# A decoder layer on one core: second buffers in the scan, other first loads, another last pass, denser decode grains

## The chip, the core and the metric

The kernel runs on one core of a Trainium2 chip. The metric is the device time of one execution in microseconds (us); three runs of the kernel before give a median and a range.

## What is computed

One step of a hybrid decoder layer, for a prompt of 512 tokens and for 8 sequences of 8 new tokens (64 sample tokens), 576 tokens in all, model width 2048, everything in 32-bit floats:

```python
mod = silu(c) @ w_ada + b_ada;  shift, scale, gate = split(mod, 3)
h = rmsnorm(x, g_pre) * (1 + scale) + shift
q, k, v, z_a, z_b, xbc, dt_raw, r_a, r_b = split(h @ w_in)
# A: three groups of dilated window attention, 8 heads of 128, (window, step) =
#    (128, 1), (512, 4), (2048, 16); the samples attend to cached keys and values too
o_a = sum_g softmax_g(lse_g) * attention_g(q, k, v);  p_a = (o_a * silu(z_a)) @ w_o_a
# B: convolution of width 4 on xbc, then a chunked state-space scan: 8 groups of 4 heads
y, new_states = ssd(xs * dt, dt * a, b, c, old_states)      # plus D skip, silu(z_b), norm
p_b = yn @ w_o_b
out = (sigmoid(r_a) * p_a + sigmoid(r_b) * p_b) @ w_o
y_out = x + gate * rmsnorm(out, g_post)
```

The outputs are y for prompt and samples, the key/value windows shifted by the new rows (some 170 MB copied), and the new convolution and scan states.

## The kernel before, in words

All large products go through 209 **units** (UNITS): a unit is one slab of 128 output columns for all 576 tokens. Units 0 to 110 are q, k, v, the gates z and r, and dt; 111 to 160 (from BLOCK0 = 111) are the slabs x and s of the scan's groups and two r; 161 to 176 (A0) multiply by w_o_a and have half the depth; then come 16 units B (w_o_b) and 16 units O (w_o). In a unit the weights are split in two parts: ACT copies the slab `raw` to `wh` (`high(u)`, line 821), POOL subtracts (`wl = raw - wh`, line 779, the tile w_lo), and PE does 3 matmuls of 288 columns for each of 16 depth steps and each of two token halves (`multiply`, lines 1156 to 1158). wh and wl have two buffers each. `raw` has three slots of 1 MB; SP loads unit u's weights (`weights`, line 432) when the low part of the unit three places before has been made (`slot_free`).

Everything else is laid over the units by **half units**: each engine's program walks `half` = 0 to 417, and what is due at a half unit stands in its queue behind that half's part of the unit. All queues run in order. SP is some halves behind its own weights (`seen`).

- **Modulation.** 32 slabs of w_ada go first, through the three slots of `raw` (`modulation`, line 1089); the small vectors v_in are waited for by PE ahead of them (line 1077). Columns of x are normalised and split (`normed`, `low`, and ACT's loop at 811 to 813), and PE starts unit 0 after all 16 (`pe.wait_ge(a_lo, KT)`).
- **Decode grains.** The samples' attention to cached keys and values is on DVE: 96 key grains and 96 value grains (`key_grain`, `value_grain`), each a product (line 1488 or 1517) and a sum (1491 or 1520) over 2048 columns. Their chunks of 1 MB come in two buffers `kd`, loaded one half ahead. `grain_half(n) = n * 16 // 17` puts 17 grains on 16 halves, the keys from half 22, the values from half 117. Then the new rows follow from half 208 (NEWS0): scores, a merge of maxima, and at half 217 (NEWV0) `value_news`, eight products (line 1534) and sums (line 1538) in one go. PE's `fold_halves` (line 1218) follows after unit 111.
- **Prompt attention** runs from half 61 to half 225 in 32 steps (head and residue class) of five halves each, with scores on PE (line 1194), a mask and a maximum on DVE (1613 to 1618), the exponential on ACT (906), transposes (1201) and the value product (1211) on PE, and 1625 and 1631 on DVE.
- **The scan.** Group g has steps o = 0 to 21, one per half from BASE[g] on, 12 halves (6 units) apart; from o = 8 on the last group goes at half that pace. PE's `outputs(g, i)` (o = 7, 9, ... 15) multiplies old states `h0T` (512 columns, line 1282), which SP loads at o = 4, 8, 10 and 12 into one buffer. For the new states POOL scales `h0` (1 MB of old states to SBUF; line 767) at o = 6 and 12, DVE adds (line 1761), and SP stores it (line 611), waits for the store, and loads the next half into the same buffer (line 606). POOL does its scan steps of a unit before the next unit's w_lo:

```python
for u in range(NU):
    pool.wait_ge(hi, u + 1)
    ...
    nc.gpsimd.tensor_tensor(wl[:, u % 2, ...], raw[...], wh[...], ALU.subtract).then_inc(lo, 1)
    ...
    for half in (2 * u, 2 * u + 1):
        for g, o in ssm_steps(half):
            ssm(g, o)
```

- **The last pass.** Units O are transposed back on PE (`back`), copied to `outs` by DVE (`copy_out`, 1854), and squared on ACT four units at a time (`squares`). After the last one DVE does `outs * rstd * gg` (line 1919) and `+ x` (line 1925) for each of five token tiles, and SP stores each.

## Time and profile before

| what | us |
|---|---|
| runs (three): median, range | 3415.59, 3413.01 to 3420.86 |
| the profiled execution: its time, its span | 3431.45, 3429.7 |
| busy PE, DVE, POOL, ACT | 3095.8, 1978.9, 1103.1, 867.8 |
| mean granted clock of TensorE | 0.944 of full speed |
| first matmul of unit 0; last matmul of unit 208 | 142.4; 3393.3 |

PE is busy for 90% of the span, DVE for 58%, POOL for 32%, ACT for 25%. Busy PE time is modelled from pipelined matmuls, and at half clock the same work shows as more busy time, so a stretch is read with its granted clock beside it. The profiled execution is 15.9 us above the median of the runs.

### The profile page before, as it was taken

Reading aid. Unit: us, or ns where it says so; the run is one execution under the profiler, and the core shown is the slowest. Engines: PE = TensorE matmul, PEld = TensorE weight load, DVE = VectorE, ACT = ScalarE, POOL = GpSimd, SP = SyncE. Lnnn points to the kernel's source line nnn. Section 1 sums busy time; section 2 is a strip of 40 time slices with the busy share of each in tenths; the row PEclk is TensorE's granted clock in tenths of the full one; section 3 lists DMA queues with packets and bytes.
Section 4 is the critical chain, followed back from the end, with each engine's and each line's share of the span. In section 5 each row is a group of like instructions: output and inputs, shape, how many; then the busy total and the mean of one; then the engine's idle time right before and its main releaser. Section 6 shows DMA issues by size and latency. Waiting matters only on the chain. (4 is left out here: it accounts for less than half of the span.)

```text
span 3429.7 us, 53566 instructions
## 1 busy us (share of the span) xinstructions
PE 3095.8 (90%) x23404; PEld 2985.7 (87%) x23404; DVE 1978.9 (58%) x1996; ACT 867.8 (25%) x1045; POOL 1103.1 (32%) x367
## 2 busy tenths in 40 slices
PE   5799999999999999989997988898887889999995
PEld 4698999899999999979996978887887878899995
DVE  3201799788857778777866466656646655211204
ACT  2111122232232222222231322322322232211221
POOL 0123333233323332233332333423324333333331
PEclk7799999999999999999998999999998989999998
DMA  8777777453537675555664455345445445766533
GB/s 304 258 260 262 304 277 254 162 198 119 172 129 256 233 266 193 194 229 207 250 230 168 176 192 176 134 175 210 155 161 203 170 148 179 266 248 243 212 137 111
DMA packets 222256, 704.94 MB, mean 206 GB/s; under 512 B 28659, under 2 KB 131819, under 8 KB 172459
## 3 DMA queue, kind: packets, MB, share of 16 engines
q1 hardware_dynamic: 159478, 471.33, 39.4%
q0 software_dynamic: 5248, 174.60, 12.6%
q10 hardware_dynamic: 57296, 55.59, 4.8%
q8 instruction: 185, 3.03, 0.4%
q14 instruction: 49, 0.40, 0.0%
HBM read 630.85 MB, written 245.17 MB: 255 GB/s over the span
## 5 line engine op out<-in xcount | busy, mean ns | idle before, releaser
L1156 PE MATMUL acc<-act,w_hi 128*128 128x288 f32 (+1 forms) x6432 | 1962.9, 305 | 141.8 <-POOL w_lo L779 134.0
L1157 PE MATMUL acc<-act,w_hi 128*128 128x288 f32 (+1 forms) x6432 | 1922.3, 299 | 0.0
L1158 PE MATMUL acc<-act,w_lo 128*128 128x288 f32 (+1 forms) x6432 | 1920.9, 299 | 0.0
L779 POOL TENSOR_TENSOR w_lo<-w_raw,w_hi 128x2048 fp32r<-128x2048 f32 (+1 forms) x209 | 968.8, 4636 | 1859.5 <-ACT w_hi L821 1844.1
L1156 PEld LDWEIGHTS acc<-act,w_hi 128*128 128x128 f32 (+1 forms) x6432 | 1233.2, 192 | 174.7 <-POOL w_lo L779 138.3
L1157 PEld LDWEIGHTS acc<-act,w_hi 128*128 128x128 f32 (+1 forms) x6432 | 1233.2, 192 | 2.8
L1158 PEld LDWEIGHTS acc<-act,w_lo 128*128 128x128 f32 (+1 forms) x6432 | 1230.4, 191 | 0.9
L821 ACT ACTIVATE w_hi<-w_raw 128x2048 fp32r<-128x2048 f32 (+1 forms) x209 | 384.1, 1838 | 407.6 <-PE acc L1158 235.4
L1517 DVE TENSOR_TENSOR side<-side 128x2048 f32<-128x2048 f32 x96 | 279.6, 2913 | 150.0 <-DMA side<-in_vals_t 142.1
L1488 DVE TENSOR_TENSOR side<-side 128x2048 f32<-128x2048 f32 x96 | 308.7, 3216 | 83.1 <-DMA side<-in_keys_t 79.0
L887 ACT ACTIVATE ev<-acc 128x576 f32<-128x576 f32 x160 | 103.7, 648 | 893.3 <-PE acc L1158 889.9
L1520 DVE TENSOR_REDUCE side<-side 128x32 f32<-128x2048 f32 x96 | 219.5, 2286 | 3.3
L1491 DVE TENSOR_REDUCE side<-side 128x16 f32<-128x2048 f32 x96 | 219.5, 2286 | 3.3
L767 POOL TENSOR_TENSOR side<-side 64x1024 f32<-64x1024 f32 x32 | 63.4, 1982 | 252.7 <-DMA side<-in_state_ssm 251.5
L1688 DVE SCALAR_TENSOR_TENSOR side<-ev,vec,side 128x511 f32<-128x511 f32 (+2 forms) x96 | 126.6, 1319 | 3.4
L1677 DVE COPY side<-side 128x24 f32<-128x24 f32 x32 | 38.9, 1214 | 151.6 <-ACT ev L887 83.6
L1826 DVE TENSOR_TENSOR ev<-acc,side 128x576 f32<-128x576 f32 x16 | 12.1, 758 | 174.7 <-PE acc L1158 174.7
L968 ACT ACTIVATE side<-side 128x512 f32<-128x512 f32 (+1 forms) x40 | 23.5, 588 | 346.0 <-DVE side L1698 346.0
L906 ACT ACTIVATE side<-side,small 128x768 f32<-128x768 f32 x32 | 30.0, 938 | 268.4 <-DVE small L1618 268.4
L1282 PEld LDWEIGHTS ps_s<-side 128*128 128x128 f32 x256 | 37.0, 222 | 61.6 <-DMA side<-in_state_t 59.5
L1282 PE MATMUL ps_s<-side 128*128 128x8 f32 x256 | 39.9, 283 | 55.9 <-DMA side<-in_state_t 55.9
L1086 PE MATMUL ps_s<-w_raw,side 128*32 128x128 f32 x1536 | 68.6, 335 | 20.1 <-DMA w_raw<-in_w_ada_t 20.1
(232 smaller groups left out, 2077.9 us busy)
## 6 DMA issues: line engine op xcount, KB each, us to landing
w_raw<-in_w_in_t SPq DMA_DIRECT2D x160, 1024.0 KB, 8.0
out_s_kv<-in_cache_a_w POOLq DMA_DIRECT2D x80, 1632.0 KB, 9.0
side<-in_keys_t SPq DMA_DIRECT2D x52, 1024.0 KB, 7.7
side<-in_vals_t SPq DMA_DIRECT2D x52, 1024.0 KB, 8.3
w_raw<-in_w_ada_t SPq DMA_DIRECT2D x48, 1024.0 KB, 7.7
out_s_kv<-in_cache_a_w POOLq DMA_DIRECT2D x24, 1344.0 KB, 8.3
w_raw<-in_w_o_b_t SPq DMA_DIRECT2D x16, 1024.0 KB, 7.6
w_raw<-in_w_o_t SPq DMA_DIRECT2D x16, 1024.0 KB, 8.7
```

The source lines that it names most:

```text
L779: nc.gpsimd.tensor_tensor(wl[:, u % 2, 0:kt, 0:cols], raw[:, s % 3, 0:kt, 0:cols], wh[:, u % 2, 0:kt, 0:cols].bitcast(F32), ALU.subtract). ...
L821: nc.scalar.activation(wh[:, u % 2, 0:kt, 0:cols], raw[:, s % 3, 0:kt, 0:cols], ACT.Copy).then_inc(hi, 1)
L887: nc.scalar.activation(ev[0:cols, c, :].rearrange("p (a n) -> p a n", a=2), banks, func).then_inc(evac, 1)
L1156: nc.tensor.matmul(out, wh[:, c, k, 0:cols], high, start=(k == 0), stop=False)
L1157: nc.tensor.matmul(out, wh[:, c, k, 0:cols], low, start=False, stop=False)
L1158: mm = nc.tensor.matmul(out, wl[:, c, k, 0:cols], high, start=False, stop=(k == kt - 1))
L1282: mm = nc.tensor.matmul(Y[:, 2 * P + j * SAMP + b * NT:2 * P + j * SAMP + (b + 1) * NT], h0T[:, b4 * P:(b4 + 1) * P], xa[:, 3, SEQ + b * N ...
L1488: TT(prod.rearrange("p (r e) -> p r e", e=E), kd[:, j % 2, :].rearrange("p (r e) -> p r e", e=E), qd[:, gi % 2, t, :].unsqueeze(1).broadca ...
L1491: TR(sc[:, t, gi, 16 * c:16 * c + 16], prod.rearrange("p (r e) -> p r e", e=E), AX, ALU.add).then_inc(d_sum, 1)
L1517: TT(prod.rearrange("p (e r) -> p e r", r=64), kd[:, j % 2, :].rearrange("p (e r) -> p e r", r=64), sc[:, t, gi, 0:64].unsqueeze(1).broadc ...
L1520: TR(og[:, 0 if gi == 2 else 1, t, 32 * c:32 * c + 32], prod.rearrange("p (e r) -> p e r", r=64), AX, ALU.add).then_inc(d_sum, 1)
L1688: STT(xp[:, lag:], ev[:, c, 0:SEQ - lag], w[3 - lag], xp[:, lag:], ALU.mult, ALU.add).then_inc(cv, 1)
```

## The change

**SP, POOL and PE in the scan.** POOL makes the low part of the *next* unit before the scan steps of this one (`weights_low`). From unit 111 to 166 weights use two slots of `raw` instead of three; the third holds a second `h0` (for the second half of a group's states) and two further `h0T` buffers (for the last group they lie in a part of `side`). `h0T` is loaded at o = 3, 5, 7 and 9, `h0` at o = 4 and 8, and no load waits for the store just issued. The decay rows (`log_decays`) move from o = 1, 3, 5, 7, 9 to 1, 3, 6, 8, 10.

**First loads.** The small vectors are loaded before the first slabs of w_ada and waited for behind the second; unit 0's weights are loaded before the last two slabs and made into wh before the last column is split; PE waits for each split column of unit 0 by itself.

**Decode grains.** Eight grains on seven halves, and the new rows' values one t at a half.

**Last pass.** The gate and norm weights are multiplied in `copy_out`; ACT squares every unit from PSUM; at the end one DVE operation a tile is left, and the samples' tile goes to ACT and POOL.

```diff
-SLOT_OF = {entry: NADA + i for i, entry in enumerate(STREAM)}
+ADA_SLOT = [n if n < NADA - 2 else n + 1 for n in range(NADA)]
+SLOT_OF = {entry: NADA + i if i else NADA - 2 for i, entry in enumerate(STREAM)}
...
+    _few = _kind == "u" and BLOCK0 <= _n < A0 + 4
+    if _few:
+        _slot = _next[1] % 2
...
+        _slot = _next[0] % 3
...
 def grain_half(n):
-    return n * 16 // 17
+    return n * 7 // 8
...
-NEWV0 = NEWS0 + 9
-FOLD0 = NEWV0 + 6
+NEWV0 = NEWS0 + 13
+FOLD0 = NEWV0 + 9
...
+        def h0(g, j):
+            buf = (xa_free if g == SG - 1 else spare)[:, 0:1024] if j else side[:, 6912:7936]
...
+        def hT_buf(g, k):
+            return k % 3 if g == SG - 1 else (4 * g + k) % 3
...
+            def slot_free(s):
+                kind, n = ENTRY[BEFORE[s]]
...
+                if kind == "u":
+                    sp.wait_ge(lo, n + 1)
+                    if KINDS[n] == "A":
+                        sp.wait_ge(ma_d, n - A0 + 1)
+                    if s == SLOT_THIRD:
+                        sp.wait_ge(yt, 5 * (SG - 1))
+                        sp.wait_ge(s_out, 32 * (SG - 1))
...
-            for n in range(3, NADA):
-                sp.wait_ge(ada_used, n - 2)
...
+            for n in range(NADA):
+                s = ADA_SLOT[n]
+                if n == NADA - 2:
+                    weights(0)
+                if s >= 3:
+                    slot_free(s)
...
+            def carried(g, k):
+                older = [(gg, kk) for gg in range(g + 1) for kk in range(4) if (gg, kk) < (g, k) and hT_buf(gg, kk) == hT_buf(g, k)]
+                if older:
+                    sp.wait_ge(yt, 5 * older[-1][0] + older[-1][1] + 1)
+                spare_free(g, hT_buf(g, k))
+                sp.dma_start(h0T(g, k), A["state_t"][g, k]).then_inc(hT_in[hT_buf(g, k)], 16)
...
             def old_states(g, j):
+                after(sp, s_out, 16 * (2 * g + j - 1))
+                spare_free(g, j)
...
-                if o in (1, 3, 5, 7, 9):
-                    log_decays(g, o // 2)
+                if o in (1, 3, 6, 8, 10):
+                    log_decays(g, (1, 3, 6, 8, 10).index(o))
...
-                if o in (4, 8, 10, 12):
-                    k = (4, 8, 10, 12).index(o)
-                    after(sp, yt, 5 * g + (k if k else -1))
-                    sp.dma_start(h0T, A["state_t"][g, k]).then_inc(hT_in, 16)
-                if o == 4 and g == 0:
+                if o in (3, 5, 7, 9):
+                    carried(g, o // 2 - 1)
+                if o == 4:
                     old_states(g, 0)
-                if o == 11:
+                if o == 8:
+                    old_states(g, 1)
+                if o == 12:
                     new_states(g, 0)
-                    sp.wait_ge(s_out, 16 * (2 * g + 1))
-                    old_states(g, 1)
-                if o == 17:
+                if o == 18:
                     new_states(g, 1)
-                    if g + 1 < SG:
-                        sp.wait_ge(s_out, 16 * (2 * g + 2))
-                        old_states(g + 1, 0)
...
-                return max(0, 2 * min(u, NGATE + 2) - 4, 2 * u - (8 if u < A0 + 3 else 4))
+                lag = 8 if u < BLOCK0 else 6 if u < A0 + 2 else 2 if u < A0 + 4 else 4
+                return max(0, 2 * min(u, NGATE + 2) - 4, 2 * u - lag)
...
             sent = 0
+            weights_low(0)
             for u in range(NU):
+                if u + 1 < NU:
+                    weights_low(u + 1)
...
+            pool.wait_ge(f_s, 1)
+            pool.wait_ge(c_in, 80)
+            nc.gpsimd.tensor_tensor(outs[4][0:SAMP, :], outs[4][0:SAMP, :], xT[4][0:SAMP, :], ALU.add).then_inc(f_p, 1)
...
+            for k in range(KT - 1):
+                split_h(k)
             high(0)
+            split_h(KT - 1)
...
-                v = u - O0
-                if v >= 5 and v % 4 == 1:
-                    squares(v // 4 - 1)
-            squares(3)
+                if u >= O0 + 2:
+                    squares(u - O0 - 2)
...
+            nc.scalar.activation(outs[4][0:SAMP, :], outs[4][0:SAMP, :], ACT.Copy, scale=fstat[0:SAMP, 4, 2:3]).then_inc(f_s, 1)
...
-                if half == NEWV0:
-                    value_news()
+                if NEWV0 <= half <= NEWV0 + NT:
+                    value_news(half - NEWV0)
...
-                TC(outP[:, :, cols], src.rearrange("p (t c) -> p t c", t=4)).then_inc(o_c, 1)
+                TT(outP[:, :, cols], src.rearrange("p (t c) -> p t c", t=4), gateP[:, cols].unsqueeze(1).broadcast_to((P, 4, P)),
+                   ALU.mult).then_inc(o_c, 1)
...
-            for t in range(5):
...
-                STT(outs[t][0:n, :], outs[t][0:n, :], fstat[0:n, t, 2:3], gg[0:n, :], ALU.mult, ALU.mult).then_inc(f_s, 1)
...
-                TT(outs[t][0:n, :], outs[t][0:n, :], xT[t][0:n, :], ALU.add).then_inc(f_d, 1)
+                STT(outs[t], outs[t], fstat[:, t, 2:3], xT[t], ALU.mult, ALU.add).then_inc(f_d, 1)
```

With this the values begin at half 111, the new rows at half 196, their values at half 209, and PE folds after unit 109.

SP's queue over one group of the scan, about the loads of group 1 (`in_state_t` is h0T, `in_state_ssm` and `out_s_ssm` are h0, `w_in_t` a unit's weights, `csT` the decay rows). Before:

```order
L455 DMA w_raw<-in_w_in_t 128x2048
L630 DMA side<-in_state_t 128x512
L648 DMA ynT<-side 128x2x576
L602 DMA side<-csT 128x4x128
L455 DMA w_raw<-in_w_in_t 128x2048
L630 DMA side<-in_state_t 128x512
L611 DMA out_s_ssm<-side 128x8x128
L606 DMA side<-in_state_ssm 128x8x128
L455 DMA w_raw<-in_w_in_t 128x2048
L630 DMA side<-in_state_t 128x512
L602 DMA side<-csT 128x4x64
```

Now:

```order
L668 DMA side<-in_state_t 128x512
L487 DMA w_raw<-in_w_in_t 128x2048
L653 DMA side<-csT 128x4x128
L674 DMA w_raw<-in_state_ssm 128x8x128
L711 DMA ynT<-side 128x2x576
L668 DMA w_raw<-in_state_t 128x512
L487 DMA w_raw<-in_w_in_t 128x2048
L653 DMA side<-csT 128x4x128
L487 DMA w_raw<-in_w_in_t 128x2048
L679 DMA out_s_ssm<-side 128x8x128
L653 DMA side<-csT 128x4x64
```

Before, each load of h0 stands right behind the store of h0 (and waits for its landing); now it stands a unit or more ahead of the store, and h0T goes out ahead of a unit's weights, not after them.

DVE's queue at the new rows' values (L1534 and L1538 before, L1620 and L1624 now, are product and sum of one t; L1613 to L1631 before are prompt attention). Before:

```order
L1534 TENSOR_TENSOR side<-side 128x1536
L1538 TENSOR_REDUCE side<-side 128x128
L1534 TENSOR_TENSOR side<-side 128x1536
L1538 TENSOR_REDUCE side<-side 128x128
L1534 TENSOR_TENSOR side<-side 128x1536
L1538 TENSOR_REDUCE side<-side 128x128
L1534 TENSOR_TENSOR side<-side 128x1536
L1538 TENSOR_REDUCE side<-side 128x128
L1525 TENSOR_TENSOR side<-side 128x1024
L1621 RECIPROCAL small<-small 128x1
L1631 TENSOR_TENSOR side<-ps_w,side 128x128
L1625 TENSOR_SCALAR side<-ps_w,small 128x128
```

Now:

```order
L1687 TENSOR_TENSOR side<-side 128x1024
L1620 TENSOR_TENSOR side<-side 128x1536
L1624 TENSOR_REDUCE side<-side 128x128
L1620 TENSOR_TENSOR side<-side 128x1536
L1624 TENSOR_REDUCE side<-side 128x128
L1712 TENSOR_SCALAR side<-ps_w,small 128x128
L1620 TENSOR_TENSOR side<-side 128x1536
L1624 TENSOR_REDUCE side<-side 128x128
L1700 TENSOR_TENSOR side<-ps_s,side 128x512
L1701 TENSOR_TENSOR side<-ps_s,side 128x256
L1703 TENSOR_REDUCE small<-side 128x1
L1705 TENSOR_SCALAR small<-small 128x1
```

Before, the eight t stand in a row and the attention's L1621 and L1631, for which PE waits, behind them; now attention's work stands between them.

## Rows read from the trace of the kernel before

**Rows 1.** Waits, whole span: who waited for whom, us, times, longest.

```profile
PE acc L1156 <- POOL w_lo L779: 134.0, 27, 9.5
...
PE ps_s L1282 <- DMA side<-in_state_t: 55.9, 15, 9.6
...
PE ps_w L1211 <- DVE side L1631: 24.1, 1, 24.1
```

**Rows 2.** Stretches: us; PE, PEld, DVE, ACT, POOL; PEclk, DMA, GB/s.

```profile
2183.50:2302.70 119.20, 104.93 (x731) 98.34 (x728) 75.46 (x128) 32.46 (x44) 41.74 (x17) 0.91 0.50 175
...
2668.20:2683.40 15.20, 15.20 (x111) 14.08 (x109) 9.18 (x17) 4.90 (x9) 6.98 (x3) 1.00 0.00 1
...
2683.40:2708.80 25.40, 16.54 (x124) 15.81 (x122) 16.96 (x25) 11.96 (x16) 9.33 (x4) 0.90 0.53 172
...
2464.20:2482.70 18.50, 18.13 (x119) 16.82 (x119) 13.30 (x29) 3.64 (x5) 5.58 (x3) 0.89 0.89 323
...
2728.60:2745.60 17.00, 16.88 (x129) 15.56 (x127) 11.65 (x24) 3.69 (x5) 4.59 (x2) 1.00 0.56 201
...
2264.40:2283.70 19.30, 15.57 (x125) 15.16 (x124) 13.85 (x20) 5.38 (x8) 8.47 (x4) 1.00 0.43 162
...
2283.70:2302.70 19.00, 18.92 (x132) 17.29 (x130) 9.93 (x16) 2.86 (x4) 5.49 (x2) 0.91 0.42 161
...
1937.00:2828.30 891.30, 766.88 (x5412) 719.76 (x5410) 530.62 (x915) 249.94 (x332) 308.82 (x128) 0.91 0.49 174
```

**Rows 3.** Timeline of POOL, 2191 to 2245 us: start, us, work, [idle before].

```profile
2214.05 3.89 POOL L767 TENSOR_TENSOR side<-side 64x1024 f32<-64x1024 f32 x2 [15.70 <-DMA side<-in_state_ssm]
...
2218.02 5.50 POOL L779 TENSOR_TENSOR w_lo<-w_raw,w_hi 128x2048 fp32r<-128x2048 f32 x1
```

**Rows 4.** Timeline of the SP queue, 2197 to 2232 us.

```profile
2199.55 1.22 SPq L611 DMA_DIRECT2D out_s_ssm<-side  x1
...
2209.64 0.38 SPq L606 DMA_DIRECT2D side<-in_state_ssm  x1
```

**Rows 5.** DVE L1688 in 1937-2828.3 us as a group; one of it.

```profile
L1688 DVE SCALAR_TENSOR_TENSOR side<-ev,vec,side 128x511 f32<-128x511 f32 (+2 forms) x84 | 113.4, 1350 | 3.0
...
2267.98 5.10 DVE L1688 SCALAR_TENSOR_TENSOR side<-ev,vec,side 128x510 f32<-128x510 f32 x1
```

**Rows 6.** Busy time at the fold (columns as in 2); DVE groups there.

```profile
1818.70:1859.10 40.40, 16.31 (x110) 13.47 (x109) 30.19 (x16) 2.57 (x2) 7.64 (x2) 0.70 0.24 88
...
L1534 DVE TENSOR_TENSOR side<-side 128x1536 f32<-128x1536 f32 x8 | 25.6, 3204 | 0.2
```

**Rows 7.** Busy time, key and value stretches (columns as in 2).

```profile
432.00:597.00 165.00, 165.00 (x1245) 164.53 (x1245) 161.29 (x54) 40.18 (x45) 57.55 (x12) 1.00 0.76 268
...
700.00:1000.00 300.00, 299.79 (x2237) 297.23 (x2236) 240.63 (x141) 87.09 (x105) 101.19 (x21) 1.00 0.44 148
...
589.00:630.00 41.00, 33.57 (x237) 32.90 (x237) 29.01 (x18) 9.73 (x12) 9.04 (x2) 0.88 0.48 177
```

**Rows 8.** DVE groups: keys 432-597 us, values 1000-1400 us.

```profile
L1488 DVE TENSOR_TENSOR side<-side 128x2048 f32<-128x2048 f32 x27 | 99.7, 3694 | 2.9 <-DVE side L1491 0.5
...
L1517 DVE TENSOR_TENSOR side<-side 128x2048 f32<-128x2048 f32 x52 | 143.6, 2762 | 94.0 <-DMA side<-in_vals_t 86.8 <-ACT side L925 6.2
```

**Rows 9.** Timelines of ACT and POOL, 125 to 147 us.

```profile
132.40 0.68 ACT L813 ACTIVATE act<-ev 128x576 fp32r<-128x576 f32 x1 [6.56 <-DVE ev L1438]
...
135.80 3.69 ACT L821 ACTIVATE w_hi<-w_raw 128x2048 fp32r<-128x2048 f32 x2
...
137.77 9.02 POOL L779 TENSOR_TENSOR w_lo<-w_raw,w_hi 128x2048 fp32r<-128x2048 f32 x2 [136.79 <-ACT w_hi L821]
```

**Rows 10.** Last pass: DVE timeline from 3399.5 us; DMA issues from 3400 us.

```profile
3400.59 2.35 DVE L1919 SCALAR_TENSOR_TENSOR side<-side,small 128x2048 f32<-128x2048 f32 x1
...
3402.97 2.29 DVE side L1925
...
out_y_prompt<-side SPq DMA_DIRECT2D x4, 1024.0 KB, 3.9
```

More of the change, by code:

```diff
@@ L306, in phase_all @@
         csr2 = side[:, 5888:6912].rearrange("p (a h n) -> p a h n", a=2, h=4)
-        h0 = side[:, 6912:7936].rearrange("p (b n) -> p b n", b=NB)
-        h0T = side[:, 7936:8448]
+        spare = raw[:, 2, :, :].rearrange("p k n -> p (k n)")
         St = side[:, 8448:8704]
@@ L332, in phase_all, with hT_loads, h0T @@
         xds = side[0:SAMP, 18168:18424].rearrange("p (h q) -> p h q", h=4)
+        xa_free = side[:, 11232:13536]
+        def h0(g, j):
+            buf = (xa_free if g == SG - 1 else spare)[:, 0:1024] if j else side[:, 6912:7936]
+            return buf.rearrange("p (b n) -> p b n", b=NB)
+        def hT_buf(g, k):
+            return k % 3 if g == SG - 1 else (4 * g + k) % 3
+        def hT_loads(g, k):
+            return sum(1 for gg in range(g + 1) for kk in range(4) if (gg, kk) <= (g, k) and hT_buf(gg, kk) == hT_buf(g, k))
+        def h0T(g, k):
+            i = hT_buf(g, k)
+            return (xa_free if g == SG - 1 else spare)[:, 512 + 512 * i:1024 + 512 * i] if i else side[:, 7936:8448]
         X, Y, Z = (ps_t, ps_w), ps_s[:, 0:512], ps_s[:, 512:1024]
@@ L412, in _ @@
             sp.dma_start(ident[:, :], A["ident"]).then_inc(c_in, 16)
-            for n in range(3):
-                sp.dma_start(raw[:, n, :, :].rearrange("p k n -> p (k n)"), A["w_ada_t"][(n % 2) * KT + n // 2]).then_inc(w_in[n], 16)
             r = 0
@@ L535, in decode_loads @@
                     new_rows(2, 0, n_in)
[L536 removed]
+                if half == NEWS0 + 10:
                     sp.wait_ge(sm_e, 1 + 2 * NT)
@@ L770, in ssm, with weights_low @@
                     pool.wait_ge(sn_m, 4 * g + 2 * j + 2)
-            sent = 0
-            for u in range(NU):
+            def weights_low(u):
                 cols = unit_cols(u)[1]
@@ L810, in _, with split_h @@
             nc.scalar.activation(root[0:SAMP, 4:5], ssq[0:SAMP, 4:5], ACT.Sqrt, bias=eps[0:SAMP, :], scale=1.0 / D).then_inc(root_done, 1)
-            for k in range(KT):
+            def split_h(k):
                 act_e.wait_ge(h_f, k + 1)
@@ L1117, in _ @@
                     modulation(n)
+                    if n == 1:
+                        vectors()
                     if n:
@@ L1150, in multiply @@
                 sl = slice(half * HALF, (half + 1) * HALF)
-                first = {A0: SPLIT_OA, B0: SPLIT_Y, O0: SPLIT_M}.get(u) if half == 0 else None
+                first = {0: 0, A0: SPLIT_OA, B0: SPLIT_Y, O0: SPLIT_M}.get(u) if half == 0 else None
                 for k in range(kt):
-                    if first:
+                    if first is not None:
                         pe.wait_ge(a_lo, first + k + 1)
@@ L1526, in merge, with value_news @@
                 dve.wait_ge(o_add, n)
-            def value_news():
-                dve.wait_ge(n_in, 64)
-                dve.wait_ge(o_add, 3)
-                for t in range(NT):
+            def value_news(t):
+                if t == 0:
+                    dve.wait_ge(n_in, 64)
+                    dve.wait_ge(o_add, 3)
+                if t < NT:
                     dve.wait_ge(n_sum, 6 + t)
@@ L1586, in softmax @@
                     dve.sem_inc(sm_x, 1)
-                if half == NEWS0 + 8:
+                if half == NEWS0 + 12:
                     dve.wait_ge(sm_w, 96)
@@ L1807, in gate_a @@
                 s, c = SLOT_OF["u", u], u % 2
-                ra = raw[:, s % 3, :, :].rearrange("p k n -> p (k n)")[:, KA * P:KA * P + TOK]
+                ra = raw[:, SLOT[s], :, :].rearrange("p k n -> p (k n)")[:, KA * P:KA * P + TOK]
                 dve.wait_ge(used, u + 1)
-                dve.wait_ge(ra_in[s % 3], 16 * sum(1 for v in range(A0, u + 1) if SLOT_OF["u", v] % 3 == s % 3))
+                dve.wait_ge(ra_in[SLOT[s]], 16 * sum(1 for v in range(A0, u + 1) if SLOT[SLOT_OF["u", v]] == SLOT[s]))
                 if n >= 2:
@@ L1903, in _ @@
                     copy_out(u - 2 - O0)
-                if half == 2 * NU - 8:
+                if half == 2 * O0 + 3:
                     dve.wait_ge(fin_in, 16 * (2 + NB))
```

194 lines of the change are left out of this document (110 added, 84 removed).

## The prediction, made before the changed kernel was run

> **What bounds the kernel now.** I read the table of waits first, then busy time cut by the unit, then timelines of the queues in the worst stretch, and last the two ends. Over the span PE waits 134.0 us for POOL's w_lo (27 times, at most 9.5), 55.9 us for the scan's old states in_state_t (15 times), and once 24.1 us for DVE's L1631 [rows 1]. So PE is the bound, and what can be won is where it waits for a part or a load. Most of that lies in one regular pattern. From 1937 to 2828.3 us PE is busy for 766.9 of 891.3 us, at a granted clock of 0.91 [rows 2].
>
> One group of the scan (six units) runs from 2183.5 to 2302.7 us: 119.2 us [rows 2]. To see what it would take unhindered I take each kind of unit where its part is busy almost all the time: x,0 15.2 us; x,1 16.5 (the busy part of a unit that took 25.4, so 8.9 us of it were idle); x,2 18.13 less the 11% of 18.5 us that its clock of 0.89 cost, 16.1; x,3 16.9; s,0 15.6; s,1 18.9 less 9% of 19.0, 17.2 [rows 2]. Together 97.5 us. The stretch holds 5412 matmuls and the group 731, so 7.4 groups [rows 2]; 7.4 x 97.5 = 722, and 169 us are lost, 23 a group.
>
> The chain behind it shows in two queues. SP issues the store of h0 (L611) at 2199.55 and, after waiting for its landing, the load of the next h0 (L606) at 2209.64 [rows 4]: ten microseconds in which the one buffer is a store's source. POOL stands idle for 15.70 us for that load, scales from 2214.05 in two pieces of 3.89 us in all, and only then makes the next unit's w_lo, from 2218.02 on, in 5.50 us [rows 3]. PE waits for that w_lo. The loads of h0T come late in the same way, since they stand behind SP's wait. After a gap PE also runs slower for a while: its granted clock is 1.00 in the undisturbed x,0 unit and 0.90 in the x,1 unit with its 8.9 idle us [rows 2], so a gap costs more than its length.
>
> **The scan, part by part.** The change takes the store's landing out of SP's way (a second h0 in the third weight slot, loads at o = 4 and 8, stores at 12 and 18), and puts w_lo of the next unit ahead of POOL's scan steps. Both have to hold, and I think that both do: a load has four halves, some 30 us, where now it has the time between a store's landing and o = 12. h0T goes out at o = 3 to 9 into three buffers, ahead of need by about two halves (16 us), where a state load of twice that size takes 4.4 us from its issue at 2209.64 to POOL's start at 2214.05 [rows 3, 4]. What is left at risk is the weights: between units 111 and 166 they have two slots, so a unit's weights are loaded after the w_lo of the unit two places before. w_lo takes 4.5 to 5.5 us, a 1 MB transfer 3.9, w_hi 1.85, the next w_lo 4.5 again [rows 3, 9, 10]: 15 to 16 us, against units of 15.2 to 17.2. POOL works a unit ahead, so this chain turns on POOL's own round and not on PE's, but there is no slack to speak of in an x,0 unit. I keep 3 us lost a group for it (bounds: 0, and 8.9 as at the x,1 unit now), and 7 us once where A begins and the lag of SP's side jobs changes. Kept: 7.4 x 3 + 7 = 29. **Scan: 169 - 29 = -140 us** (ends -169 and -100).
>
> **Fold.** value_news puts eight products of 3.2 us and their sums in one go on DVE; L1631 stands behind them, and the window from 1818.7 to 1859.1 is one unit that took 40.4 us with PE busy 16.3 at a clock of 0.70 [rows 1, 6]. At full clock those 16.3 us would be about 14 (estimate, between 16.3 x 0.70 = 11.4 and 16.3). One t a half leaves attention's work between them. **Fold: -26 us.** Nine halves instead of one carry about 5 us more of DVE work each; DVE is busy 30.2 of those 40.4 us now, so the same work, spread over nine halves of 7 to 8 us, is cover that suffices unless attention's steps fill them (then a few gaps of 2 to 3 us; end -15).
>
> **Denser grains.** This is the term that goes against the change. In the key stretch before attention, DVE is busy 161.3 of 165 us while PE is never idle, and 27 grains start in it [rows 7, 8]: 6.0 us a grain, nearly full. Eight on seven halves instead of seventeen on sixteen is 7.6% more, 29.0 grains in the same 165 us, or 173 us of work. Over the 39 halves from 22 to 61 it adds three grains, so 18 us of lag, when the first attention step comes; already now PE is idle 7.4 of the 41 us there, at a clock of 0.88 [rows 7]. Behind that, halves are longer: from 700 to 1000 us DVE is busy 240.6 of 300 with 40 grains [rows 7], and 3 more at 5 to 6 us make 256, so that the lag is worked off. I take 12 us more gap once, plus 3 for the clock after it. In the value stretch DVE waits 86.8 us for chunks while it makes 52 grains [rows 8]; there the rate is set by loads and DVE has time. **Grains: +15 us** (ends -10, if the chunk waits that reach PE become fewer, and +45, if three steps stall in place of one).
>
> **The first loads.** Now the last column is split at 132.40 in 0.68 us, w_hi of units 0 and 1 follow at 135.80 (3.69 for two), w_lo of unit 0 is done 4.5 us after 137.77, and PE starts at 142.4 [rows 9]. With w_hi of unit 0 ahead of the last split it can start at 133.1, w_lo ends at 133.1 + 1.85 + 4.5 = 139.5: 2.8 us. The vectors no longer stand before PE's first sum; another 1.2 us from the stream of w_ada (ends 5, and -3 since unit 0's megabyte, 3.9 us [rows 10], now goes ahead of the last two slabs). **Head: -4 us.**
>
> **The last pass.** Five tiles of 2.35 + 2.29 us [rows 10] are 23.2 us; four of 2.35 are 9.4: 13.8 less. The samples' tile costs 1.9 us on ACT (as a w_hi) and at most 4.5 on POOL (as a w_lo) beside them [rows 9]. But the four stores of 1 MB take 3.9 us each [rows 10]; one after another they are 15.6 us, and then only 9 us are saved. **Tail: -10 us** (ends -13.8 and -9). The Trainium skill, "SBUF — State Buffer", section "Who interferes with whom", says that a DVE instruction with two SBUF inputs contends with a GpSimd instruction that reads SBUF, and that the loser waits for the whole instruction; by it POOL's addition of 4.5 us would stand in DVE's way and the saving would be 9.3. That the gate's multiplication moves into the copies from PSUM, and the squares to one unit at a time, I cost at nothing: beside them ACT has little but one w_hi of 1.85 us a unit [rows 9] and DVE no grains or scan any more; without that cover `back`, which now waits for the squares of two units before, would hold PE for a microsecond or so in each of 16 units, 16 us.
>
> **Sum.** -140 - 26 + 15 - 4 - 10 = -165 on the profiled execution's 3431.45, so 3266.5. That execution is 15.9 us above the median 3415.59; the forecast for the median is **3250 us**.
>
> **Rivals.** *The prefetch does not come early* (the change does not do what it says): SP's queue runs in order, each h0T now waits for an earlier `yt`, and two weight slots leave SP waiting for POOL; a late weight load then holds back every state load. For it: the 15 to 16 us round above. Against: w_lo is now made ahead of the scan's steps. If half of the 169 us stays, 85 instead of 29, the time is 3306. *DVE becomes the bound of the scan.* It is busy 75.5 of the 119.2 us of a group [rows 2], which would be 75.5 of 97.5. One L1688 took 5.10 us where the mean of 84 is 1.35 [rows 5], at a time when POOL was busy 8.47 us in one unit with its scaling and w_lo [rows 2]; such a block on DVE did not stop PE then, since PE was late itself. With the slack gone, two blocks of 8.5 us a group and 3 us of clock would, 20 us x 7.4 = 148, less the 22 already kept: 3376. The rule of the Trainium skill named above, in "SBUF — State Buffer", "Who interferes with whom", is this mechanism; the 5.10 us agrees with it, but is one instruction. *The denser grains never let DVE catch up* (the other side): prompt attention has 32 steps, and if DVE's lag stays above the two halves or so that a step can bear, each step stalls PE as the first one does now, 7.4 us and 2 of clock [rows 7]. It decides once DVE's work in the attention stretch passes its time, which needs 60 us more in 300 where I count 16. With 27 of the 32 steps stalled, 3250 - 15 + 27 x 9 = 3478, slower by 1.8%.
>
> **How the numbers follow.** Forecast 0.81, prefetch late 0.08, DVE the bound 0.05, grains' stall 0.03, others 0.03 (a new wait in the A units, most likely, 20 to 60 us above the forecast). The forecast's own range is 3205 to 3290: all of the scan's 29 us and a gain from the grains at one end, the scan at -100 at the other. With the first rival's 3306 it is 3200 to 3306. A measurement of this kernel tells about 0.2% (7 us) from no change; faster by more than that has all but the third rival, 0.96, the same 0.01, slower 0.03.
>
> **What would show it.** In the changed profile: POOL's wait for in_state_ssm and PE's for in_state_t gone or under 10 us together; a group of the scan at 98 to 103 us with a clock near 1.00; no wait of 24 us for the attention's product after unit 109; a first attention step with some 12 us more idle time than now; the first matmul near 138 us; 25 to 27 us from the last matmul to the end. The forecast is wrong if the scan's groups stay above 110 us, if PE waits for DVE at more than three attention steps, or if w_lo stays the largest releaser of PE with tens of waits.

## The result, and the profile after

The changed kernel takes 3334.84 us (median of four runs, 3333.79 to 3336.43) against 3418.23 for the kernel before in the same comparison (3413.01 to 3427.05): a ratio of 0.9754, interval 0.9732 to 0.9776. It is faster by 83 us; the forecast said 165, and the time lies above its range, which ended at 3306. The profiled executions, 3336.43 and 3431.45 us, differ by 95.0; of those 13 stem from the one before lying above its own median. The forecast's 165 was for this pair, so it missed by 70 us: 52 at the grains, 11 in the scan, 8 in the A units, and the rest smaller and partly against each other.

The table splits the two profiled executions at the first matmul of a unit. "Gap" is time in which PE did nothing.

| stretch | before | after | change | forecast |
|---|---|---|---|---|
| start to unit 0 | 142.4 | 130.0 | -12.4 | -4 |
| units 0 to 29 | 432.0 | 435.3 | +3.3 | 0 |
| units 30 to 60 | 477.0 (gap 13.1) | 509.2 (gap 36.1) | +32.2 | +15 |
| units 61 to 109 | 767.3 (gap 41.1) | 802.4 (gap 62.7) | +35.1 | (in the +15) |
| unit 110, the fold | 40.4 | 13.9 | -26.5 | -26 |
| units 111 to 160, the scan | 969.2 | 840.1 | -129.1 | -140 |
| units 161 to 176 (A) | 134.9 | 143.2 | +8.3 | 0 |
| units 177 to 208 | 430.4 | 430.3 | 0 | 0 |
| after the last matmul | 36.1 | 30.2 | -5.9 | -10 |

Busy time by stretch in the changed kernel (columns as in [rows 2]): units 30 to 60, 61 to 109, the fold's unit, units 116 to 160, and one group of the scan, the one after that of [rows 2]:

```profile
565.30:1074.50 509.20, 473.11 (x3415) 465.53 (x3412) 400.42 (x225) 137.49 (x177) 151.73 (x31) 0.96 0.49 172
1074.50:1876.90 802.40, 739.73 (x5289) 728.23 (x5289) 578.43 (x356) 215.04 (x241) 252.11 (x74) 0.96 0.57 206
1876.90:1890.80 13.90, 13.90 (x110) 11.76 (x110) 0.95 (x2) 1.54 (x1) 5.08 (x2) 1.00 0.54 199
1967.80:2730.90 763.10, 739.08 (x5419) 692.59 (x5418) 493.64 (x915) 245.47 (x326) 302.56 (x128) 0.98 0.59 202
2154.90:2256.70 101.80, 99.21 (x730) 92.90 (x730) 69.37 (x128) 32.57 (x44) 40.30 (x17) 0.98 0.57 197
```

The group that answers to 119.2 us at a clock of 0.91 now takes 101.8 at 0.98, and the fold's 24.1 us wait is gone [rows 2, 6]. But units 30 to 109, with their matmuls unchanged, are 67 us longer. PE's waits over the whole span of the changed kernel:

```profile
PE acc L1245 <- POOL w_lo L845: 79.0, 24, 10.6
...
PE ps_s L1290 <- ACT side L982: 22.4, 4, 13.9
PE ps_s L1393 <- DVE side L1834: 19.5, 7, 3.3
```

There is no wait for in_state_t any more and the 134.0 us for w_lo are 79.0 [rows 1], but these stand elsewhere: none in the scan's groups, most of it between units 30 and 114. L982 is the exponential of a prompt attention step. One of the forecast's signs of being wrong is there: w_lo is still PE's largest releaser, with 24 waits.

How w_lo, which is POOL's, comes late in an attention step can be followed at unit 51. DVE, then ACT, POOL and PE, each in its own timeline of the changed kernel (start, us, work, idle before and what ended it):

```profile
898.94 6.38 DVE L1573 TENSOR_TENSOR side<-side 128x2048 f32<-128x2048 f32 x1 [9.64 <-DMA side<-in_keys_t]
...
912.32 2.29 DVE L1573 TENSOR_TENSOR side<-side 128x2048 f32<-128x2048 f32 x1
914.65 2.29 DVE L1576 TENSOR_REDUCE side<-side 128x16 f32<-128x2048 f32 x1
916.85 0.35 DVE L1712 TENSOR_SCALAR side<-ps_w,small 128x128 f32<-128x128 f32 x1
917.11 2.29 DVE L1573 TENSOR_TENSOR side<-side 128x2048 f32<-128x2048 f32 x1
919.43 2.29 DVE L1576 TENSOR_REDUCE side<-side 128x16 f32<-128x2048 f32 x1
...
923.67 0.15 DVE L1705 TENSOR_SCALAR small<-small 128x1 f32<-128x1 f32 x1
```

```profile
923.86 0.94 ACT L982 ACTIVATE side<-side,small 128x768 f32<-128x768 f32 x1 [14.04 <-DVE small L1705]
...
924.79 1.89 ACT L897 ACTIVATE w_hi<-w_raw 128x2048 fp32r<-128x2048 f32 x1
```

```profile
926.76 4.51 POOL L845 TENSOR_TENSOR w_lo<-w_raw,w_hi 128x2048 fp32r<-128x2048 f32 x1 [23.59 <-ACT w_hi L897]
```

```profile
931.33 0.61 PE L1245 MATMUL acc<-act,w_hi 128*128 128x288 f32 x1 [3.09 <-POOL w_lo L845]
```

DVE, held by a chunk's load until 898.94, works off grains one behind the other and comes to the mask and maximum (the last is L1705) at 923.67. The first product took 6.38 us and not 2.29; POOL's w_lo, from 898.60 on for 4.58 us, ran beside it. ACT has stood for 14 us at the exponential, and w_hi of the next unit stands behind it in ACT's queue; POOL's w_lo waits for that, and PE for w_lo. The wait is charged to POOL, and the work behind it is the grains ahead in DVE's queue, together with the late chunk and the slow product; e4 below moves the grains and nothing else.

### The profile page after: what moved, and what is told of

It is laid out like the page before. It is cut to its first block, busy times and chain, and to the rows that moved or that the text cites. A ratio compares the mean times of both kernels' runs of the same rounds, so it can differ in the third digit from the quotient of the medians.

```text
span 3334.7 us, 53699 instructions
## 1 busy us (share of the span) xinstructions
PE 3082.8 (92%) x23404; PEld 2970.4 (89%) x23404; DVE 1931.1 (58%) x1990; ACT 883.3 (26%) x1166; POOL 1093.6 (33%) x368
## 4 chain that ended last, share of the span: by engine, by line
PE 59%; DVE 13%; DMA 10%; issue 9%; POOL 5%; ACT 2%; SPq 1%; ACTq 0%; DVEq 0%; POOLq 0%
PE acc L1245 18%; PE acc L1246 17%; PE acc L1247 17%; POOL w_lo L845 5%; DVE side L1602 3%; DVE side L1775 2%; DMA side<-in_vals_t 2%; DMA side<-in_state_conv_t 2%; DMA w_raw<-in_w_ada_t 2%; ACT w_hi L897 1%; PE ps_s L1172 1%; DMA side<-in_keys_t 1%; DVE side L1776 1%; DVE side L1605 1%; DVE side L1573 1%
## 5 line engine op out<-in xcount | busy, mean ns | idle before, releaser
L845 POOL TENSOR_TENSOR w_lo<-w_raw,w_hi 128x2048 fp32r<-128x2048 f32 (+1 forms) x209 | 955.2, 4571 | 2195.7 <-ACT w_hi L897 2195.5
L1602 DVE TENSOR_TENSOR side<-side 128x2048 f32<-128x2048 f32 x96 | 282.3, 2941 | 134.7 <-DMA side<-in_vals_t 132.7
L1573 DVE TENSOR_TENSOR side<-side 128x2048 f32<-128x2048 f32 x96 | 315.4, 3285 | 74.8 <-DMA side<-in_keys_t 70.6
L1775 DVE SCALAR_TENSOR_TENSOR side<-ev,vec,side 128x511 f32<-128x511 f32 (+2 forms) x96 | 171.2, 1783 | 3.4
L982 ACT ACTIVATE side<-side,small 128x768 f32<-128x768 f32 x32 | 30.0, 938 | 328.1 <-DVE small L1705 328.1
L1172 PE MATMUL ps_s<-w_raw,side 128*32 128x128 f32 x1536 | 66.2, 326 | 27.5 <-DMA w_raw<-in_w_ada_t 27.2
L1172 PEld LDWEIGHTS ps_s<-w_raw,side 128*32 128x32 f32 x1536 | 49.0, 130 | 35.8 <-DMA w_raw<-in_w_ada_t 22.0
L1764 DVE COPY side<-side 128x24 f32<-128x24 f32 x32 | 16.4, 514 | 108.8 <-ACT ev L963 62.9
L906 ACT ACTIVATE side<-ps_t 128x512 f32<-128x512 f32 x48 | 28.5, 594 | 145.5 <-PE ps_t L1257 145.5
L1776 DVE SCALAR_TENSOR_TENSOR side<-side,vec 128x64 f32<-128x64 f32 x96 | 60.8, 633 | 0.0
```

What stands on the lines that cost most here:

```text
L845: nc.gpsimd.tensor_tensor(wl[:, u % 2, 0:kt, 0:cols], raw[:, SLOT[s], 0:kt, 0:cols], wh[:, u % 2, 0:kt, 0:cols].bitcast(F32), ALU.subtract ...
L1172: mm = nc.tensor.matmul(ps_s[q:q + 32, (n % 2) * 512:(n % 2) * 512 + P], c32[:, k, :], raw[:, SLOT[src], k, :], start=(k < 4), stop=(k >= ...
L1573: TT(prod.rearrange("p (r e) -> p r e", e=E), kd[:, j % 2, :].rearrange("p (r e) -> p r e", e=E), qd[:, gi % 2, t, :].unsqueeze(1).broadca ...
L1602: TT(prod.rearrange("p (e r) -> p e r", r=64), kd[:, j % 2, :].rearrange("p (e r) -> p e r", r=64), sc[:, t, gi, 0:64].unsqueeze(1).broadc ...
L1775: STT(xp[:, lag:], ev[:, c, 0:SEQ - lag], w[3 - lag], xp[:, lag:], ALU.mult, ALU.add).then_inc(cv, 1)
```

## The experiments

All were timed in three rounds beside the kernel before (medians 3417.4, 3418.2, 3419.2 and 3413.8 us in the four comparisons). "Attention" is units 30 to 60 and 61 to 109, "fold" units 110 to 113, "scan" units 116 to 160, all from one profiled execution.

| kernel | median | ratio of medians (95% interval) | attention | fold | scan |
|---|---|---|---|---|---|
| before | | | 477.0 + 767.3 | 80.5 | 892.3 |
| after | 3334.8 | 0.9754 (0.9732-0.9776) | 509.2 + 802.4 | 52.2 | 763.1 |
| e1 before, dense grains | 3497.5 | 1.0234 (1.0213-1.0255) | 510.6 + 824.8 | 52.2 | 898.7 |
| e2 after, sparse grains | 3268.8 | 0.9563 (0.9544-0.9581) | 474.3 + 758.5 | 70.2 | 761.2 |
| e3 after, new rows later | 3312.3 | 0.9689 (0.9667-0.9712) | 509.9 + 777.0 | 53.9 | 759.7 |
| e4 after, attention first | 3232.7 | 0.9462 (0.9438-0.9485) | 477.2 + 728.8 | 52.2 | 760.8 |
| e5 after, POOL's old order | 3410.0 | 0.9971 (0.9957-0.9985) | 509.6 + 802.2 | 52.2 | 837.5 |
| e6 before, attention first | 3349.1 | 0.9795 (0.9775-0.9816) | 464.0 + 719.2 | 67.1 | 892.7 |
| e7 = e4, sparse | 3198.7 | 0.9356 (0.9336-0.9375) | 464.0 + 710.3 | 66.4 | 759.3 |
| e8 = e4, D weights, tail | 3219.7 | 0.9421 (0.9399-0.9442) | 475.7 + 734.4 | 52.2 | 761.4 |
| e9 before, POOL's new order | 3291.7 | 0.9627 (0.9608-0.9645) | 474.4 + 755.8 | 79.2 | 779.4 |
| e10 = e8, 12 grains on 11 | 3211.8 | 0.9397 (0.9381-0.9413) | 469.1 + 731.5 | 54.0 | 761.9 |
| e11 after, loose halves | 3302.8 | 0.9662 (0.9644-0.9680) | 495.0 + 779.2 | 52.2 | 764.0 |
| e12 = e7, tail | 3191.4 | 0.9342 (0.9309-0.9375) | 458.5 + 710.2 | 66.6 | 758.8 |

**e1, e2: what density costs.** One line in either kernel:

```diff
-    return n * 16 // 17
+    return n * 7 // 8
```

e1, on record before it ran: 

> The kernel before with eight grains on seven halves and nothing else changed (new rows, their values and the fold follow 12 halves earlier). Theory D (density is what the forecast mis-sized): units 30 to 109 get about 50 to 65 us longer, and the total is about 50 us above that of the kernel before, some 3465 us. Rival P (the forecast's +15 was right for the grains alone, and the added gaps of the changed kernel come from its new queue orders): about +15 us, 3430. Either way the scan's groups stay at 119 to 123 us.

e2 is the other way round (new rows' offsets as before, their values two a half): 

> The changed kernel with 17 grains on 16 halves; the new rows' values come two t at a half over four halves. Theory D: units 30 to 109 fall by 50 to 65 us, the total by about 55 us to 3280, with up to 10 us of gap back at the fold. Rival P: 3320, since most of the added gaps stay.

Both speak for density, and it cost more than I expected: +80 us on the kernel before, -66 without it in the changed one. The attention stretch is 91 us longer in e1 and 79 shorter in e2. The +15 of the forecast is too small by a factor of four to six (67, 79 or 91 us). In e1 the fold costs nothing, but the 27.6 us wait for L1625 stands at unit 103, which took 42.6 us:

```profile
1776.60:1819.20 42.60, 14.95 (x106) 14.47 (x105) 41.71 (x20) 3.21 (x2) 6.95 (x2) 0.71 0.36 139
```

DVE is busy for 41.71 of 42.60 us: the eight products and sums in one go hit whatever attention step follows. The changed kernel has nothing of the kind, so the spreading of the values, and not the earlier fold, took the 26 us away; in e2, with two t a half, 14.6 us of gap are back at unit 111.

**e4, e6: the place of attention in DVE's queue.** In e4 one call moves up, and nothing is added or left out; e6 does the same to the kernel before:

```diff
+                attention(half)
                 for n in grains.get(half - KEYS0, ()):
                     key_grain(n)
...
                     value_news(half - NEWV0)
-                attention(half)
```

> The changed kernel with attention's operations ahead of the grains of the same half on DVE. Theory B (gaps come from one or two grains, 5 to 14 us, in front of a step's operation): most gaps of units 30 to 109 go, 40 to 60 us less, some 3285. Rival: DVE then waits for PE's scores before it may start its grains, loses its lead, and the next half's operations are as late as before: 3325 to 3350.

> The kernel before with attention's operations ahead of the grains and of the new rows' values of the same half on DVE; nothing else. If the place of attention in DVE's queue is what makes the gaps of units 30 to 109 at the old density too, about 35 to 50 us less there (they have 53.7 us of gaps, some of which are waits for loads), 3370 to 3385 in total, the fold's gap and the scan as before. If those gaps come from a lag that attention's place does not change, within 10 us of 3417.

e4 is 102 us faster than the changed kernel (40 to 60 were expected), all of it in the attention stretch (-105.6), more than density had added. The rival, that DVE would lose its lead by waiting for PE, is out. e6 wins 69 us on the kernel before, at its old density, where 35 to 50 were expected. In the stretch of units 61 to 109, e6 reads:

```profile
1031.00:1750.20 719.20, 711.78 (x5273) 705.23 (x5273) 619.44 (x358) 214.69 (x239) 252.34 (x75) 1.00 0.67 244
```

DVE is busy for 86% of that stretch and PE loses 7 us; in the changed kernel DVE is busy for 72% and PE loses 63 (above). So DVE's mean load in the stretch does not tell how long PE waits. What counted was what stood ahead of attention's operations in its queue.

**e11: mean load or bursts.** As many grains on as many halves, but a half with two grains is moved by 0 to 4 halves to one in which attention has nothing for DVE:

```diff
+    double = {next(h for h in range(d, d + 5) if h < ATT0 or (h - ATT0) % 5 == 2) for d in range(base, base + 84, 7)}
```

> The changed kernel with as many grains on as many halves (96 on 84, twelve halves with two), but from half 61 on each half with two grains is moved on, by 0 to 4 halves, to one in which attention has no operation on DVE (the third of its five). Theory B (a half with two grains right in front of attention's operations makes the gaps, not the mean load): the gaps of units 61 to 109 fall from 62.7 us to 35 or less, with their clock 30 to 45 us less in all, 3290 to 3305. Rival M (the mean load of DVE): within 8 us of 3335.

The total came within the range of theory B, 32 us less, but not wholly in the way it says: the gaps of units 61 to 109 fall from 62.7 to 47.2 us, not to 35. So the doubled halves explain a part, about 37 of the 79 us between e2 and the changed kernel (14.2 in units 30 to 60, 23.2 in units 61 to 109). One long gap is left in e11, that of the next run.

**e3: one coincidence.** Two halves' shift of the new rows, their values and the fold:

```diff
-NEWS0 = VALS0 + grain_half(NGR) + 1
+NEWS0 = VALS0 + grain_half(NGR) + 3
```

> The changed kernel with the new rows two halves later (half 198 and not 196), so that the wait for their load does not stand ahead of the first operation of an attention step. Theory N (the longest added gap, 13.9 us at unit 99 and 5.5 behind it with their slow clock, is that wait's place): 15 to 23 us less, 3312 to 3320. Rival (DVE is late there by the grains' own lag): no change within 5 us.

22.5 us less, as theory N had it. At the changed kernel's half 196, a multiple of five behind 61, the new rows' first products stand right ahead of an attention step's first operation. DVE there, in the changed kernel:

```profile
1694.47 2.29 DVE L1584 TENSOR_TENSOR side<-side 128x2048 f32<-128x2048 f32 x1 [11.54 <-DMA side<-rows]
...
1710.73 2.29 DVE L1588 TENSOR_REDUCE side<-side 128x16 f32<-128x2048 f32 x1
1712.94 0.68 DVE L1700 TENSOR_TENSOR side<-ps_s,side 128x512 f32<-128x512 f32 x1
```

11.5 us of waiting for the rows and 18.5 us of work on them, then the scores' mask (L1700). PE stood for 13.9 us at unit 99 and 5.5 at unit 100. The kernel before had the new rows at 208, two halves into a step, without such a gap.

**e5, e9: what won the scan's time.** e5 takes POOL's new order back in the changed kernel, e9 gives it to the kernel before, with one h0, one h0T and its late loads (there the low part is first made a function; e5 is the same diff read backwards):

```diff
+            weights_low(0)
             for u in range(NU):
-                weights_low(u)
+                if u + 1 < NU:
+                    weights_low(u + 1)
...
-                            pool.wait_ge(lo, u + 1)
+                            pool.wait_ge(lo, min(u + 2, NU))
```

> The changed kernel, but POOL makes the low part of a unit behind the scan steps of the unit before, as in the kernel before; the buffers and loads stay as changed. Theory L (what cost the time in the scan was waiting for loads, so the buffers alone win it): the scan's units 116 to 160 stay within 15 us of 763, the total within 15 us of 3335. Rival O (POOL's 8.5 us of scaling and w_lo in a row is itself late for PE): 5 to 9 us a gap, one or two gaps a group, 60 to 100 us more, 3400 to 3430.

> The kernel before, with POOL making the next unit's low part ahead of this unit's scan steps, and its one h0 buffer and late loads as they are. If order and buffers win separate things (w_lo's gaps of 9 us a group by the order, in_state_t's waits by the buffers), the scan's units 116 to 160 fall from 892 to 820 to 850 us and the total to 3350 to 3375. If the order only helps once loads are early, since POOL's wait of 15 us for h0 then comes ahead of the w_lo after next and DVE and PE wait for the states instead, the total stays within 15 us of 3418.

This is the finding of the study. With no new buffer e9's scan falls from 892.3 to 779.4 us, 113 of the 129 us. (That e9 is also 43 us faster than the changed kernel in all is no merit of its scan: it keeps the old density of grains, and its attention stretch is 81 us shorter.) The buffers and early loads add 16 (763.1). In the other order they are worth more, 55 us (892.3 to 837.5): in large part both act on the same waits, and what the one has taken away the other cannot take again. Both branches of e9's expectation are wrong. PE's waits in units 116 to 160 of the kernel before:

```profile
PE acc L1156 <- POOL w_lo L779: 63.4, 7, 9.5
PE ps_s L1282 <- DMA side<-in_state_t: 55.9, 15, 9.6
```

In e9 PE waits for no w_lo there, and its gaps fall from 124 to 32 us:

```profile
1936.00:2828.30 892.30, 767.88 (x5419) 720.73 (x5417) 531.29 (x919) 250.56 (x333) 308.82 (x128) 0.91 0.49 174
```

```profile
1914.30:2693.70 779.40, 747.53 (x5418) 701.16 (x5417) 494.98 (x915) 245.57 (x327) 301.44 (x128) 0.97 0.57 199
```

The groups of POOL's work from 1937 to 2828 us in the kernel before, then in e9:

```profile
L767 POOL TENSOR_TENSOR side<-side 64x1024 f32<-64x1024 f32 x30 | 59.1, 1971 | 243.9 <-DMA side<-in_state_ssm 242.8
```

```profile
L767 POOL TENSOR_TENSOR side<-side 64x1024 f32<-64x1024 f32 x32 | 64.5, 2015 | 17.1 <-DMA side<-in_state_ssm 15.7
```

The load of h0 is as late in the program as ever, and still POOL hardly waits for it. e9's POOL:

```profile
2102.07 4.70 POOL L779 TENSOR_TENSOR w_lo<-w_raw,w_hi 128x2048 fp32r<-128x2048 f32 x1 [15.71 <-ACT w_hi L827]
...
2107.27 3.92 POOL L767 TENSOR_TENSOR side<-side 64x1024 f32<-64x1024 f32 x2
```

and SP's queue:

```profile
2093.72 0.39 SPq L611 DMA_DIRECT2D out_s_ssm<-side  x1
...
2097.23 0.38 SPq L606 DMA_DIRECT2D side<-in_state_ssm  x1
```

The low part of the next unit waits for its w_hi, which comes about a unit later than that of this unit did. POOL so spends the same idle time in front of a w_lo that PE does not need yet, and reaches the scaling of h0 when the load has landed. In the kernel before the 15.70 us stood behind w_hi, with a w_lo that could have been made [rows 3]. The largest wait left to e9's scan is PE's for in_state_t, 24.1 us in 11 times instead of 55.9 in 15 [rows 1]; this is what the buffers took. The order also changed DVE's time: the two rows of stretches above have DVE busy for 531 and 495 us with the same operations, and how much of the 113 us goes through that was not separated.

e5 came out where rival O put it, 75 us above the changed kernel, so the buffers alone do not win the scan. But the mechanism is not O's: PE waits for no w_lo there, and 72.0 of its 75.0 us of gaps in the scan are charged to DVE, 5.3 to 7.1 us at most x,1 units and 4.8 at the x,3. The queues of SP, DVE and POOL at unit 130, which starts at 2220.6 us in e5:

```profile
2220.19 0.43 SPq L646 DMA_DIRECT2D side<-in_state_conv_t  x1
```

```profile
2229.08 0.18 DVE L1762 COPY side<-side 128x24 f32<-128x24 f32 x1 [7.28 <-DMA side<-in_state_conv_t]
...
2235.20 4.52 DVE L1774 SCALAR_TENSOR_TENSOR side<-side,vec 128x64 f32<-128x64 f32 x1
...
2240.93 0.42 DVE L1804 TENSOR_TENSOR side<-side 64x256 f32<-64x256 f32 x1
```

```profile
2230.76 3.97 POOL L833 TENSOR_TENSOR side<-side 64x1024 f32<-64x1024 f32 x2 [10.51 <-DMA side<-in_state_ssm]
2234.81 4.83 POOL L845 TENSOR_TENSOR w_lo<-w_raw,w_hi 128x2048 fp32r<-128x2048 f32 x1
```

PE's wait of 5.65 us ends behind that L1804. Two things hold DVE. SP's loads stand behind a unit's weights, and these wait for w_lo; in the old order the load of in_state_conv_t goes out 0.4 us before the unit starts, in the changed kernel 7.3 us before, and from its issue to DVE's start it is some 9 us in both. Then L1774 (0.28 us where POOL does nothing) takes 4.52 beside POOL's scaling and w_lo. At x,3 the two stand in a row again, and DVE's operations of 0.75 us take up to 4.98 beside them.

**e7, e8, e10, e12: towards the fastest.** e7 is e2 and e4 together. 

> Attention first on DVE and 17 grains on 16 halves, with all else of the change. If attention first takes away what density costs, density then no longer matters, and this is within 10 us of the 3233 of the dense one, apart from 15 us at the fold, where the new rows' values come two t at a half: 3235 to 3250. If density costs a part of its own (DVE's lag at the first step), units 30 to 109 come out 10 to 20 us shorter, and the total near 3225.

e8 is e4 with these edits, and the samples' operations of ACT and POOL taken out; e12 is e7 with the second of them:

```diff
-                            sp.dma_start(dsk[64 * hh:64 * hh + 64, :], A["d_skip"][0:1, hh:SH:2].to_broadcast((64, KT))).then_inc(const_in, 16)
+                            sp.dma_start(dsk[64 * hh:64 * hh + 64, :], A["d_skip"][0:1, hh:SH:2].to_broadcast((64, KT))).then_inc(dk_in, 16)
...
+            STT(outs[4][0:SAMP, :], outs[4][0:SAMP, :], fstat[0:SAMP, 4, 2:3], xT[4][0:SAMP, :], ALU.mult, ALU.add).then_inc(f_p, 1)
```

> Attention first, and two further edits. The scan's D weights get a semaphore of their own, so that the dt part no longer waits for their many small descriptors: the gap of 10.5 us at unit 114 and about 2 us of clock go. The samples' last operation stands on DVE as the fifth, and not on ACT and POOL: if POOL's addition is what made three operations take 11.1 us and not 7.1, five now take 11.8 us (13.4 before), and the last store is the small one, so the tail falls from 30.2 to 26 or 27 us. Total 3233 - 12 - 3 = 3218. Rival for the tail: the stores set its end, and it stays at 29 to 31.

e10 is e8 with `n * 11 // 12` for `n * 7 // 8`, and the new rows' offsets of the kernel before, but the values one t a half and the fold four halves later than there:

> The changed kernel with attention first on DVE, 12 grains on 11 halves, the new rows' values one a half, a semaphore of its own for the scan's D weights, and the samples' last operation on DVE. From the sparse one with attention first (3199): the gap of 8.4 us at unit 111 and about 4 us of clock go, 4.4 us less at the tail, and up to 8 us back for the denser grains: 3182 to 3192. It would be wrong above 3200.

> Attention first, 17 grains on 16 halves, and the samples' last operation on DVE. Against the same kernel with that operation on ACT and POOL (3199): the tail falls from 30.2 to 25.8 us as it did beside the dense grains, so 3194 to 3196, and nothing else moves. Wrong if the total is above 3203.

e7 has next to no gap from unit 61 to 109 (0.3 us), and comes out 34 us faster than e4, not within 10: with attention first, density still costs DVE's lag at the first step (8.2 us at unit 31 against 3.7) and a few w_lo gaps. e8 did as expected: with a semaphore of their own for the D weights the gap at unit 114 goes (units 114 and 115 take 27.2 us after 39.1; in e7 they take 27.2 with the shared semaphore, DVE waiting 3.0 us for the D weights and not 14.3 as in the changed kernel, so it is the sharing together with the dates that costs), and the tail falls from 30.2 to 25.8. e10 missed its bound, 3212 for at most 3200. It took the gap at unit 111 away (12 us), but units 61 to 109 are 21 us longer than in e7, with new waits of 3.4, 5.3 and 6.6 us at units 81, 90 and 103; which of its shifted dates makes them was not tried. e12 has the tail of 25.8 us by itself, 4.4 less. In its total it is 7 us below e7, but the intervals of the two ratios overlap, so the total does not show the gain and the tail does. It is the fastest kernel here: 3191.4 us, 222 below the kernel before in its comparison and 143 below the changed one.

## Why the prediction was right in direction and wrong in size

- **The scan, -140: measured -129.** The size held, the reason only in part. The text said that "both have to hold", the store's landing out of the way and w_lo ahead of the scan's steps. e9 shows that the second does 113 of 129 us by itself. The floor of 97.5 us a group was sound: 101.8 in the profile, of which each group keeps a gap of about 3 us at unit x,3, PE waiting for L1834. The 3 us a group that the sum kept for the weight slots came, but not from them: PE waits for no w_lo in units 116 to 160. They are the rival "DVE becomes the bound of the scan" in small. In six of the seven groups the operation L1775 just ahead of L1834 takes 5.0 us beside POOL's w_lo, where it takes 0.75 without POOL. At unit 132 of the changed kernel (DVE, POOL, PE):

```profile
2237.82 4.99 DVE L1775 SCALAR_TENSOR_TENSOR side<-ev,vec,side 128x510 f32<-128x510 f32 x1
...
2244.42 0.42 DVE L1834 COPY side<-ps_s 128x256 f32<-128x256 f32 x1
```

```profile
2237.55 4.71 POOL L845 TENSOR_TENSOR w_lo<-w_raw,w_hi 128x2048 fp32r<-128x2048 f32 x1 [10.90 <-ACT w_hi L897]
```

```profile
2244.98 0.66 PE L1393 MATMUL ps_s<-side 64*128 64x512 f32 x1 [2.51 <-DVE side L1834]
```

- **The fold, -26: measured -26.5**, by the cause named (e1 shows the stall to move with the values when they stay in one go).
- **The grains, +15: the step that failed.** Measured +67 in the attention stretch between the two kernels, +91 in e1, 79 back in e2. The step set DVE's mean work against the time, found it enough ("256 of 300") and let only the first attention step pay. The stated range took the scan's bad end and left out the grains' own +45; with both it would have reached 3320, still short. The first attention step paid what was said, about: units 30 and 31 are 9.3 us longer. The rest came where the mean load says nothing, at later attention steps: one or two grains of 4.6 to 9 us, at unit 51 behind a late chunk, ahead of an operation for which ACT, POOL and PE wait in turn. There are 24 halves with two grains now, 12 before. I had seen the same chain in the fold and did not look for it in small. e11 puts 32 us of it on the doubled halves, e3 22.5 on the new rows' date, and e4, with attention first, takes back the whole and more.
- **The rival on the slower side** had the right mechanism and the wrong point: I asked for DVE to be overfull by 60 us in 300, and attention steps stalled at 72% busy. Without the scan's gain it would have decided, as e1 does: 1.0234.
- **The head, -4: measured -12.4** in the pair of profiles. Kernels with the old first loads began unit 0 at 136.3 to 142.4 us (before, e1, e6, e9), those with the new at 130.0 to 133.0, so some 8 us are the change's. I had taken 1.2 us for the vectors' place. In the kernel before PE waited 13.1 us for them once, with the stream of w_ada stopped for want of a slot.
- **The tail, -10: measured -5.9.** Three of DVE's operations took 11.1 us, not 7.0:

```profile
3312.26 11.12 DVE L2011 SCALAR_TENSOR_TENSOR side<-side,small,w_raw 128x2048 f32<-128x2048 f32 x3
```

```profile
3314.33 4.62 POOL L865 TENSOR_TENSOR side<-side 64x2048 f32<-64x2048 f32 x1 [27.40 <-ACT side L1149]
```

POOL's addition lies inside them. In e8, where the addition is DVE's own, the same group reads:

```profile
3200.91 6.88 DVE L2006 SCALAR_TENSOR_TENSOR side<-side,small,w_raw 128x2048 f32<-128x2048 f32 x3
```

4.2 us less for three, which is POOL's 4.6 within a little. The rule of the Trainium skill that was weighed there ("SBUF — State Buffer", "Who interferes with whom") gave a saving of 9.3 us for DVE's operations; they saved 9.6 (13.4 us from the first to the end of the last, where five pairs took 23.0), so the trace agrees. The sum lost the rest behind them: a store of 1 MB is last now and not one of 512 KB, 9.0 us from its operation's end to the end of the span instead of 6.1.
- **Units A, 0: measured +8.3**, all of it at unit 161 (18.6 us, was 10.1), where PE waits for DVE's parts of the attention output. e9, with the old slots and the old dates for SP, takes 134.1 us for the A units, but unit 161 is long there too (16.4 us); it makes up for it at units 165, 166 and 176. So slots and dates do not explain most of unit 161. The kernel before had lost 9.1 us just in front of it, at the end of unit 160, which may have given DVE that time; this was not tried, nor what costs the changed kernel 9 us against e9.

## What to carry to other kernels

Where engines run in order, a wait costs what stands behind it: before adding a buffer for a late load, move the work that does not need it ahead of the wait. Put the operations for which a chain of engines waits ahead of the filler in each slot of the schedule, and judge a denser schedule by its worst slot and not by the mean load of the engine. When a wait is charged to an engine that has been idle for long, follow its queue back to what stood in front.
